# The third tile's last sum is turned by halves before its norm, and its closing squares are formed by quarters

## The reference, cut to what matters

```python
for i in range(DEPTH):                                   # DEPTH = 2
    h = h + mix                                          # a recurrent mixer
    h = h + _peer(_rmsnorm(h, norm_ffn[i]), ...)         # 8 heads x 16 experts a token, by gathered rows
    gate = sigmoid(_rmsnorm(h, norm_ple[i]) @ w_ple_gate[i] + b_ple_gate[i])
    h = h + gate * (p[i] @ w_ple_proj[i])
y = _rmsnorm(h, norm_final)
# _rmsnorm(x, g) = x * rsqrt(mean(x*x) + EPS) * g
```

## Time and profile before

| | us |
|---|---|
| median of 3 runs | 2510.52 (2509.81 to 2511.47) |
| the profiled execution, its own time | 2502.38 |
| its span | 2500.80 |

### The profile page before, as it was taken

One profiled execution on the slowest core, in us unless ns is written; L12 is line 12 of the kernel. 1 busy time (PEld: TensorE's weight loads), 2 busy tenths in 40 slices (PEclk: granted clock), 3 DMA queues, 4 the chain that ended last, 5 costly groups with the idle time before them and its releaser, 6 DMA issues.

```text
span 2500.8 us, 22276 instructions
## 1 busy us (share of the span) xinstructions
PE 2142.7 (86%) x6952; PEld 1219.3 (49%) x6952; DVE 1447.2 (58%) x3602; ACT 692.5 (28%) x1641; POOL 1316.3 (53%) x1387
## 2 busy tenths in 40 slices
PE   7998989889888877789779998898897798787797
PEld 5667664444334433335456686654443344333354
DVE  1445336566676766676315463365666767666763
ACT  3323223222223331223223232222222223312232
POOL 2013136676777777777100131366677777777771
PEclk9998999999889999989889989999899999888998
DMA  7320079999999999999373201799999999999993
GB/s 226 105 83 24 28 272 341 405 404 406 409 409 409 409 409 409 409 407 406 125 205 101 87 20 51 272 344 404 406 406 409 409 409 405 409 409 409 409 392 134
DMA packets 260983, 761.96 MB, mean 305 GB/s; under 512 B 26973, under 2 KB 91413, under 8 KB 260861
## 3 DMA queue, kind: packets, MB, share of 16 engines
q0 software_dynamic: 188480, 686.97, 70.1%
q1 hardware_dynamic: 72380, 73.50, 9.2%
HBM read 751.66 MB, written 8.72 MB: 304 GB/s over the span
## 4 chain that ended last, share of the span: by engine, by line
PE 46%; DMA 28%; POOL 11%; DVE 7%; issue 5%; ACT 2%; SPq 0%; DVEq 0%; ACTq 0%; POOLq 0%
PE ps L1690 45%; DMA arena<-in_peer_u_dram,idx_u 27%; POOL arena L722 6%; POOL arena L716 5%; DVE arena L1294 3%; DMA wring<-in_w_in_dram 1%; ACT arena L1101 1%; PE ps L1706 0%; DVE xn L1630 0%; DVE wgt L1302 0%; ACT xn L999 0%; DVE arena L1568 0%; DVE arena L1555 0%; DMA h<-in_x_sample_dram 0%; DVE arena L1571 0%
## 5 line engine op out<-in xcount | busy, mean ns | idle before, releaser
L1690 PE MATMUL ps<-arena 128*128 128x512 f32 (+5 forms) x3808 | 1423.4, 529 | 271.5 <-ACT arena L1101 249.5
L1690 PEld LDWEIGHTS ps<-arena 128*128 128x128 f32 (+3 forms) x3808 | 671.6, 204 | 972.5 <-issue 903.2
L1294 DVE CUSTOM_DVE_ANT_0 arena<-arena,ps 128x1024 f32<-128x1024 f32 x640 | 779.7, 1221 | 528.4 <-DMA arena<-in_peer_u_dram,idx_u 508.3
L722 POOL DMA_INDIRECT arena<-in_peer_v_dram,idx_u x640 | 608.0, 950 | 297.0 <-PE ps L1690 160.3
L716 POOL DMA_INDIRECT arena<-in_peer_u_dram,idx_u x640 | 607.8, 950 | 273.5 <-issue 174.5
L1690 PE MATMUL ps<-aT,wring 128*128 128x320 f32 (+2 forms) x1344 | 371.6, 432 | 12.2 <-ACT aT L1008 4.9
L1094 ACT ACTIVATE gelu<-hid 128x4 f32<-128x4 f32 x160 | 32.9, 206 | 1103.3 <-DVE hid L1294 1103.2
L1690 PEld LDWEIGHTS ps<-aT,wring 128*128 128x128 f32 x1344 | 254.5, 197 | 135.6 <-issue 45.4
L1690 PE MATMUL ps<-wring,aT 128*128 128x256 f32 x960 | 224.6, 388 | 3.9 <-ACT aT L1066 2.6
L1690 PEld LDWEIGHTS ps<-wring,aT 128*128 128x128 f32 x960 | 182.0, 193 | 51.9 <-issue 25.7
L1101 ACT ACTIVATE arena<-ident,wgt 128x128 f32<-128x128 f32 x512 | 163.4, 390 | 73.8 <-DVE wgt L1302 72.4
(11 more groups left out here) (297 smaller groups left out, 1355.3 us busy)
## 6 DMA issues: line engine op xcount, KB each, us to landing
wring<-in_w_in_dram SPq DMA_DIRECT2D x28, 1024.0 KB, 5.8
wring<-in_w_peer_q_dram SPq DMA_DIRECT2D x18, 1024.0 KB, 11.8
arena<-in_peer_u_dram,idx_u POOLq DMA_INDIRECT x640, 13.1
arena<-in_peer_v_dram,idx_u POOLq DMA_INDIRECT x640, 13.1
wring<-in_w_out_dram SPq DMA_DIRECT2D x8, 1024.0 KB, 5.3
wring<-in_w_ple_gate_dram SPq DMA_DIRECT2D x8, 1024.0 KB, 17.6
arena<-in_state_gdn_dram POOLq DMA_DIRECT2D x2, 2048.0 KB, 18.5
out_dram<-arena POOLq DMA_DIRECT2D x2, 2048.0 KB, 11.9
```

The costliest lines, as they stand in the source:

```text
L722: pool.indirect_dma_start(vrow[:, n % G, :], None, v_l, bass.IndirectOffsetOnAxis(ap=at, axis=0)).then_inc(v_loaded[n % G], 16)
L1294: dve.tensor_tensor_reduce(out=urow[:, n % G, :], in0=urow[:, n % G, :], in1=x_bank, scale=1.0, scalar=0.0, op0=ALU.mult, op1=ALU.add, acc ...
L1690: return pe.matmul(out, lhsT, rhs, start=start, stop=stop, skip_group_check=True)
```

## The change

The third tile's `h` itself is transposed, without its norm: DVE adds the last sum in two halves of 512 columns, and PE turns four pieces as soon as each half is there. ACT and DVE put on `norm_ple` as before. The gate products start from zero, with neither the norm's factor nor the bias in them; the factor (one number a token) is formed meanwhile. Behind each block DVE multiplies the product with that factor and adds the bias (`scalar_tensor_tensor`, into `sig`), and ACT takes the sigmoid of `sig`. So the bias is wanted on all 128 partitions, and SP loads it as a broadcast. After each block's addition DVE forms the sum of squares of that quarter; behind the fourth it adds the four numbers up and forms the mean. ACT, behind the fourth sigmoid, takes a root of a constant into an unused place, ahead of the wait for the mean. Two semaphores (`par_ready`, `hist_ready`) become counts of one (`opened`); that is left out below.

```diff
+        ssq_part = sb("ssq_part", [P, 4])
...
-                sp.dma_start(bias_row, row(b_ple_gate, layer)).then_inc(rows_loaded, 16)
+                sp.dma_start(gain_row[:, :], row(b_ple_gate, layer).to_broadcast([P, D])
+                             ).then_inc(rows_loaded, 16)
...
                 def square(i):
-                    act.wait_ge(h_added, i + 1)
+                    act.wait_ge(h_added, i + 1 if i < 2 else 4)
...
+                turn(2)
                 square(2)
                 root(2)
-                turn(2)
                 for m in range(4):
-                    embed(2, m)
-                next_square(2)
-                next_root(2)
+                    act.wait_ge(ple_biased, m + 1)
+                    act.activation(sig[:, m % 2, :], sig[:, m % 2, :], ACT.Sigmoid
+                                   ).then_inc(ple_sig, 1)
+                act.activation(rstd[:, 3:4], eps[:, 0:1], ACT.Sqrt)
+                act.wait_ge(var_ready, TILES + 2 * TILES)
+                act.activation(rstd[:, 2:3], ssq[:, 2:3], ACT.Sqrt).then_inc(std_ready, 1)
...
             def add_sum(i):
...
+                else:
+                    for b in range(2):
+                        c = slice(BANK * b, BANK * (b + 1))
+                        dve.tensor_tensor(h[:, i, c], h[:, i, c], bank(ACC_BANK[i] + b), ALU.add
+                                          ).then_inc(h_added, 1)
...
             def turn_half():
-                dve.wait_ge(xT_done, KD + 2 * TILES)
+                dve.wait_ge(xT_done, KD + 2 * TILES + 1)
...
                 add_sum(2)
+                turn_half()
                 mean(2)
-                rescale(2, own)
-                turn_half()
+                dve.wait_ge(std_ready, TILES + 5)
+                own.after(dve.reciprocal(rstd[:, 2:3], rstd[:, 2:3]))
+                own.settle()
+                dve.wait_ge(rows_loaded, 32)
                 for m in range(4):
+                    c = slice(WCOLS * m, WCOLS * (m + 1))
+                    dve.wait_ge(ple_mm, 9 + m)
+                    dve.scalar_tensor_tensor(sig[:, m % 2, :], gate_of(2, m), rstd[:, 2:3],
+                                             gain_row[:, c], ALU.mult, ALU.add
+                                             ).then_inc(ple_biased, 1)
                     embed(2, m, own)
-                next_mean(2)
+                    dve.wait_ge(ple_done, 9 + m)
+                    own.after(dve.tensor_tensor_reduce(
+                        out=xn[:, 2, c], in0=h[:, 2, c], in1=h[:, 2, c], scale=1.0, scalar=0.0,
+                        op0=ALU.mult, op1=ALU.add, accum_out=ssq_part[:, m:m + 1]))
+                own.settle()
+                own.after(dve.tensor_reduce(ssq[:, 2:3], ssq_part[:, :], AX, ALU.add))
+                own.settle()
+                dve.tensor_scalar(ssq[:, 2:3], ssq[:, 2:3], 1.0 / D, EPS, ALU.mult, ALU.add
+                                  ).then_inc(var_ready, 1)
                 next_scale(2, own)
...
+                for b in range(2):
+                    pe.wait_ge(h_added, 3 + b)
+                    for k in range(4 * b, 4 * b + 4):
+                        ins = pe.transpose(heads(TURN_BANK[2] + b)[:, k % 4, :],
+                                           h[:, 2, P * k:P * (k + 1)], ident[:, :])
+                    ins.then_inc(xT_done, 1)
                 pe.wait_ge(u_free, G + NSTEP * TOPK)
                 pe.wait_ge(ple_done, 8)
+                pe.wait_ge(aT_ready, KD // 2 + 3 + TILES)
                 for m in range(4):
-                    offset(2, m)
-                turn(2)
-                for m in range(4):
-                    embed(2, m, 0)
-                    embed(2, m, 1)
+                    for k in range(KD):
+                        if m == 0 and k == 4:
+                            pe.wait_ge(aT_half, KD // 2 + 1)
+                        ins = mm(gate_of(2, m), aT[:, k, P * 2:P * 3],
+                                 wring[:, (B_PLE + m) % RING, k, :], k == 0, k == KD - 1)
+                    ins.then_inc(ple_mm, 1)
                 meet(pe, layer)
```

More of the change, by code:

```diff
@@ L342, in hybrid_trunk @@
         first_T = lsem("first_T")
-        par_ready = lsem("par_ready")
+        opened = lsem("opened")
+        ple_biased = lsem("ple_biased")
         pT_ready = lsem("pT_ready")
-        hist_ready = lsem("hist_ready")
         sq_done = lsem("sq_done")
@@ L759, in gained @@
             def gained():
-                act.wait_ge(par_ready, 1)
+                act.wait_ge(opened, 1)
                 for k in range(0, KD, 2):
@@ L828, in evacuate @@
                         if f == 0:
-                            act.wait_ge(hist_ready, 1)
+                            act.wait_ge(opened, 2)
                         act.activation(raw[:, f, 0:SEQ], ps[:, b, 0:SEQ], ACT.Copy)
@@ L1137, in gained @@
             def gained():
-                dve.wait_ge(par_ready, 1)
+                dve.wait_ge(opened, 1)
                 for k in range(1, KD, 2):
@@ L1306, in add_sum @@
                 dve.wait_ge(v_free, G + TOPK * sum(STEPS[:i + 1]))
-                dve.tensor_tensor(h[:, i, :], h[:, i, :],
-                                  ps[:, ACC_BANK[i]:ACC_BANK[i] + 2, :].rearrange("p a b -> p (a b)"),
-                                  ALU.add).then_inc(h_added, 1)
+                if i < 2:
+                    dve.tensor_tensor(h[:, i, :], h[:, i, :],
+                                      ps[:, ACC_BANK[i]:ACC_BANK[i] + 2, :].rearrange(
+                                          "p a b -> p (a b)"), ALU.add).then_inc(h_added, 1)
+                else:
[3 more added lines that the diff above has]
+                                          ).then_inc(h_added, 1)
             def mean(i):
@@ L1362, in _ @@
                 dve.wait_ge(first_T, 1)
-                dve.tensor_copy(par[:, :], ps[:, 7, 0:76]).then_inc(par_ready, 1)
+                dve.tensor_copy(par[:, :], ps[:, 7, 0:76]).then_inc(opened, 1)
                 gained()
@@ L1371, in _ @@
                                           .rearrange("p (b j) -> p b j", b=NB))
-                ins.then_inc(hist_ready, 1)
+                ins.then_inc(opened, 1)
                 dve.wait_ge(small_loaded, 80)
@@ L1782, in _ @@
                     if n == 2:
-                        pe.wait_ge(hist_ready, 1)
+                        pe.wait_ge(opened, 2)
                     if n == 3:
@@ L2167, in embed @@
                             pe.wait_ge(rows_loaded, 32)
[L2168 to L2174, removed]
+                        if n >= 2:
+                            pe.wait_ge(ple_done, n - 1)
+                        project(i, m)
+                        offset(i, m)
                     for k in range(2) if part == 0 else range(2, KD):
```

## The result

| | us |
|---|---|
| changed kernel, median of 6 runs | 2493.69 (2485.89 to 2496.14) |
| kernel before beside it, median of 6 | 2509.97 (2504.94 to 2511.47) |
| ratio | 0.9937, 95% interval 0.9922 to 0.9952 |
| profiled execution after, its own time (span) | 2492.08 (2490.60) |

The two profiled executions differ by 10.3 us (2502.38 and 2492.08), the medians by 16.3.

A forecast was written before the change was run, and what follows sets the result against it. Memory traffic of 404 to 409 GB/s was taken to bound the expert stages, a one-engine chain the tails. 8.2 + 3.0 + 2.2 - 2.5 = 10.9 us off the 2510.52 median gave 2499.7, range 2494.5 to 2505.5.

The forecast's parts named there:

- Step 1: Both layers' tails: first gate product starts 2.61 us behind the sum's start, saving 8.2 us together.
- Step 2: The tails' 64 gate products: one fall to half clock in two layers, 13.81 us at full clock; saves 3.0 us.
- Step 3: Closing norm: scaling starts 3.17 us behind the last product, Sqrt table load hidden; saves 2.2 us in two layers.
- the drain: Rival at ACT's table switch: about 1380 ns extra, step 3 saves 0.1 instead of 2.2, time 2501.8; chance 0.02.
- Step 4: Bias broadcast in the saturated expert stage: 508 KB more cost 1.27 us a layer, 2.5 us lost.
- A hidden broadcast: Expert stage: idle turns take the broadcast's packets at no cost; part of the 2495.3 us case, chance 0.15.
- gathers that stand still: Slower rival in the expert stage: broadcast stops the gathers, up to 13.1 us a layer, 2523.3 us; chance 0.03.
- The kind rival: No clock fall in either tail and the broadcast hidden: 15.2 us saved, 2495.3 us; chance 0.15.
- Two signs: Third tile's sum about 1.3 us later in the first layer; second layer's expert stage 1.3 us longer.
- a sign of being wrong: For the expert stages: the prediction is wrong if one grows by more than 3 us.

The follow-up runs named there:

- the filled pauses: Kernel before with unread products put into PE's two tail pauses and the fourth bias product moved ahead of its block: median 2501.55 us, ratio 0.9982.
- the broadcast alone: Kernel before with only the bias load changed to a 512 KB broadcast to 128 partitions, PE still reading its first row: median 2510.27 us, ratio 1.0004.
- the closing alone: Kernel before with only the squares by quarters, early root of a constant and last root; norm, turn and bias as before: median 2502.95 us, ratio 0.9994.
- the third run of the changed kernel: Changed kernel unedited, timed again beside the kernel before on another chip: median 2496.09 us of 6 runs, ratio 0.9962 to the kernel before.
- nine-fold run: Changed kernel with the bias broadcast nine times a layer instead of once: median 2513.47 us, ratio 1.0025 to the kernel before, 19.8 above the changed kernel.

## Why the prediction was right in its steps and wrong in its range

**Step 1, right.** The first product at 2.72 and 2.73 us (forecast 2.61), 8.0 gained (forecast 8.2). The hand-overs and the end of the transposes took 0.1 more than I had written.

**Step 2, right mechanism, mis-sized term.** I took one fall of the clock in two tails and a gain of 3.0. The first trace had none: 4.3 gained (16.84 and 15.58 against 14.05 twice; without any fall I would have forecast 4.8, since I took the 64 products for 13.81). One fall in 12 tails is what the runs show, at 1.69, near the 1.77 I had taken. That the loss before came from the stretch without products is shown by the filled pauses. What I hadn't seen is that the clock also falls ahead of the sum, in some tails of either kernel, where it costs the same 1.69.

**Step 3, right.** 3.20 behind the last product (forecast 3.17), 2.1 gained (2.2). The table load took 1.28 with nothing behind it, here as before: the root of the constant follows it by 0.01. So the drain that the Trainium skill adds to a switch of tables (page "ScalarE: Activation LUTs", section "What ACT_TABLE_LOAD costs") isn't seen in this trace either, and that rival falls.

**Step 4, right mechanism, size perhaps high.** 2.5 forecast; 1.24 a transfer by sixteen of them, so 2.5 for two. The stages themselves give 0.91 for a single one, so 1.8 for two, with 2.5 near the edge of what the standard error allows. A hidden broadcast and gathers that stand still both fall. The kind rival was thus half right: its other half, no fall behind the sum in either tail, came true in the first trace. Two signs that I had named for this step can't be read from one trace: the first layer's sum came 3.79 later and not 1.3, and its stage from the first gather to the sum grew by 3.19 (885.33 against 882.14), over the 3 us that I had called a sign of being wrong. 1.69 of that is the clock ahead of the sum; in the second layer the same stage shrank by 0.35.

**Sum.** By the traces 8.0 + 4.3 + 2.1 - 2.5 = 11.9 against 10.9, or 12.6 with the 1.8 of the stages. The mean of six traced tails with the old turn and closing (27.3; two are from the broadcast alone) and of ten after (20.1, the one fall in it) gives the same 14.4 for the tails. All timed runs of the four sets together: 69 of the kernel before have a mean of 2506.9 and a spread (standard deviation) of 3.7, 18 of the changed kernel 2494.2 and 3.3. The difference is 12.7, with a standard error of about 0.9 (the root of 3.7²/69 + 3.3²/18). So nothing outside the tails and the broadcast is needed, and none was found: the 16.3 of the first comparison was partly chance. One thing stays open: side by side the medians differ by 16.3, 14.3 and 9.8 in the three comparisons, which is wider than 0.9 lets expect, so something may differ between the sets that wasn't tested.

**What failed** is the base that the sum was taken from: "I carry this difference over unchanged" and "The runs before spread by 0.8 either way". Three runs between 2509.81 and 2511.47 looked like a firm base. Over 69 runs the kernel before lies between 2497.93 and 2513.45, so that base was 3.6 above the mean. Nor was the 8.14 between profile and median a property of profiling: in eleven sets of the changed kernel and the experiments the profiled run lies between 3.7 below and 3.1 above its set's median. It was draws from this spread, the profile a low one, the three runs high ones. 2506.9 less the forecast 10.9 is 2496.0, inside the range; from 2510.5 it came out 3.6 higher, and the range, which allowed the base no error, ended 0.8 above the result. Of the 6.0 us between forecast and result 3.6 are the base; 1.3 are step 2's term (3.0, measured 4.3), up to 0.7 step 4's. The rest is inside the scatter. So the range was missed by the base first, and the mis-sized clock term went the same way.

**Where the scatter lies** can be read from the 13 traces. Tails of one kernel repeat to 0.1 us but for the clock. The clock ahead of the sum adds 1.69 or nothing. The stage from the first gather to the sum, less that, lies between 883.5 and 884.1 in the 12 cases with one broadcast. What moves most is the mixer's part ahead of the first gather: from 333.2 to 337.9 us in the first layer and from 334.2 to 341.4 behind the last scaling in the second. PE's clock is a part of it. This is that stretch in the second layer, in the closing alone and in the third run of the changed kernel (columns as in the earlier trace rows):

```profile
1246.49:1580.72 334.23, 299.24 (x1505) 227.46 (x1506) 139.89 (x334) 95.15 (x180) 45.28 (x28) 0.94 0.32 94
1243.07:1583.90 340.83, 305.27 (x1505) 232.66 (x1506) 139.99 (x334) 95.16 (x180) 45.28 (x29) 0.92 0.31 92
```

The same 1505 instructions keep PE busy 6.03 us longer at the lower granted clock, and the stretch is 6.60 longer; DVE's, ACT's and POOL's busy times agree to 0.1. What makes the clock differ from run to run wasn't tried.

## What to carry to other kernels

A norm's factor commutes with the product behind it, so the turn and the products can start on the raw sum, and the norm runs beside them; what that needs elsewhere (here a bias on all partitions) is priced by the stage it lands in. In one bound by its bytes the bytes are the estimate, and here they came out at 1.24 of 1.28 us in the nine-fold run and 0.9 in single ones. Shortening a stretch without products paid twice here, 8.0 us in waiting and 4.3 in the clock; filling it paid in the clock alone. And a base of three runs is no base: before a sum of small terms is put on a median, ask how far single runs of that kernel lie apart, the profiled one among them. When a change's gain is smaller than that spread, measure from the traces the stages that it touches: the tails repeat to 0.1 us where the runs spread by 3.7.

## What the runs showed of the hardware that was not expected

The same 2.7 us between the last gathered row's products and the first gate product, with the same transposes in it, left the clock at 2.4 GHz in eleven tails and brought it to 1.2 GHz in one (PEclk 0.68 in the microsecond from 1223, 0.50 after it, 0.61 from 1226). In ten of the eleven it had been at 1.2 GHz among the rows' products before, and had risen again ahead of the sum. 512 KB broadcasts from one 4 KB row, one after the other, cost no more than other bytes: 1.24 us each, against 1.28 for 512 KB at 409 GB/s.
